# Decoder layer on one core: first copies of the down-projection's weight sums moved to SP's queue in the attention stages, the adding transfers spread singly, the residual loaded in four parts

## The reference

```python
def hybrid_layer(x, ...):
    h = rms_norm(x, norm_mix_pre)
    q, k, v, u, gate_a, gate_s = jnp.split(h @ w_in, IN_SPLITS, axis=-1)
    ...                      # three groups of dilated attention, an S5 state-space branch
    merged = jax.nn.sigmoid(gate_a) * attn_branch + jax.nn.sigmoid(gate_s) * ssm_branch
    x = x + rms_norm(merged @ w_out, norm_mix_post)
    h = rms_norm(x, norm_ffn_pre)
    f = (jax.nn.silu(h @ w_ffn_gate) * (h @ w_ffn_up)) @ w_ffn_down     # D_FF = 5632
    return x + rms_norm(f, norm_ffn_post)
```

## Time and profile before

| | us |
|---|---|
| median of three runs | 2716.58 |
| the profiled execution | 2715.48 |
| its span | 2713.6 |
| PE busy in it | 2629.2 (97%) |
| DVE busy | 1749.2 (64%) |
| ACT busy | 1059.6 (39%) |
| POOL busy | 529.0 (19%) |

### The profile page before, as it was taken

One profiled execution on the slowest core, in us unless ns is written; L12 is line 12 of the kernel. 1 busy time (PEld: TensorE's weight loads), 2 busy tenths in 40 slices (PEclk: granted clock), 3 DMA queues, 4 the chain that ended last, 5 costly groups with the idle time before them and its releaser, 6 DMA issues.

```text
span 2713.6 us, 38844 instructions
## 1 busy us (share of the span) xinstructions
PE 2629.2 (97%) x14213; PEld 2234.7 (82%) x14213; DVE 1749.2 (64%) x2209; ACT 1059.6 (39%) x1427; POOL 529.0 (19%) x825
## 2 busy tenths in 40 slices
PE   8999999999999999999997999999999998999998
PEld 7888888888888888888876878888888887888886
DVE  5333332243345999923756898988989996666677
ACT  5222322233323444522523443434344443555554
POOL 3978037750000000001011110111101000000000
PEclk9999999999999999999998999999999999999999
DMA  6444663344434445466477878778787656777776
GB/s 180 140 144 130 121 194 99 97 120 130 164 123 140 148 139 169 164 220 178 159 222 210 241 205 239 215 210 245 206 241 207 191 170 241 241 241 244 239 242 222
DMA packets 305219, 504.19 MB, mean 186 GB/s; under 512 B 28976, under 2 KB 238256, under 8 KB 302352
## 3 DMA queue, kind: packets, MB, share of 16 engines
q1 hardware_dynamic: 251784, 319.62, 36.5%
q0 software_dynamic: 36032, 164.62, 22.4%
q10 hardware_dynamic: 17288, 18.40, 2.0%
HBM read 448.60 MB, written 150.41 MB: 221 GB/s over the span
## 4 chain that ended last, share of the span: by engine, by line
PE 63%; issue 28%; POOL 4%; DMA 2%; DVE 2%; ACT 1%; ACTq 0%; DVEq 0%; SPq 0%; POOLq 0%
PE ps L494 8%; PE ps L498 8%; PE ps L496 8%; PE ps L785 7%; PE ps L849 5%; PE ps L851 5%; PE ps L853 5%; PE ps L791 3%; POOL v_d L2865 2%; PE ps L615 2%; PE ps L616 2%; PE ps L617 2%; POOL v_d L2862 1%; DMA v_d<-in_w_ffn_down 1%; PE ps L600 1%
## 5 line engine op out<-in xcount | busy, mean ns | idle before, releaser
L482 DVE TENSOR_TENSOR w_lo<-raw,w_hi 128x1024 fp32r<-128x1024 f32 x176 | 229.8, 1306 | 538.2 <-ACT w_hi L478 538.1
L478 ACT ACTIVATE w_hi<-raw 128x1024 fp32r<-128x1024 f32 x176 | 186.4, 1059 | 558.1 <-PE ps L498 346.5
L494 PE MATMUL ps<-a_both,w_hi 128*128 128x512 f32 x640 | 252.3, 394 | 0.0
L496 PE MATMUL ps<-a_both,w_hi 128*128 128x512 f32 x640 | 249.3, 389 | 0.0
L498 PE MATMUL ps<-a_both,w_lo 128*128 128x512 f32 x640 | 249.2, 389 | 0.0
L785 PE MATMUL ps<-a_both,w_hi 128*128 128x512 f32 x872 | 223.7, 399 | 6.0 <-DVE f_sg L2480 5.3
L785 PEld LDWEIGHTS ps<-a_both,w_hi 128*128 128x128 f32 x872 | 163.0, 192 | 41.6 <-issue 7.1
L785 PE MATMUL ps<-a_both,w_hi_b 128*128 128x512 f32 x640 | 163.4, 398 | 3.3 <-ACT w_hi_b L715 2.1
L715 ACT ACTIVATE w_hi<-raw 128x1024 fp32r<-128x1024 f32 x81 | 85.7, 1058 | 185.8 <-DVE raw L2171 82.7
L2891 POOL DMA_DIRECT2D fs_d<-f_sums x22 | 14.0, 637 | 736.9 <-DVE f_sums L2443 736.9
L785 PEld LDWEIGHTS ps<-a_both,w_hi_b 128*128 128x128 f32 x640 | 119.2, 192 | 30.5 <-issue 4.1
(11 more groups left out here) (440 smaller groups left out, 6556.7 us busy)
## 6 DMA issues: line engine op xcount, KB each, us to landing
v_d<-in_w_ffn_down POOLq DMA_DIRECT2D x132, 512.0 KB, 10.0
raw<-in_w_in SPq DMA_DIRECT2D x108, 512.0 KB, 4.1
raw<-in_w_ffn_gate SPq DMA_DIRECT2D x88, 512.0 KB, 18.5
raw<-v_d SPq DMA_DIRECT2D x88, 512.0 KB, 4.8
raw_b<-in_w_ffn_up SPq DMA_DIRECT2D x80, 512.0 KB, 6.0
raw<-in_w_ffn_down SPq DMA_DIRECT2D x66, 512.0 KB, 4.9
v_d<-v_d POOLq DMA_DIRECT2D x44, 512.0 KB, 13.9
raw<-in_w_out SPq DMA_DIRECT2D x32, 512.0 KB, 4.6
```

What stands on the lines that cost most here:

```text
L478: nc.scalar.activation(w_hi[:, m % 2, :], raw[:, m % 4, :], ACT.Copy).then_inc(hi_ready, 1)
L482: nc.vector.tensor_tensor(w_lo[:, m % 2, :], raw[:, m % 4, :], w_hi[:, m % 2, :].bitcast(F32), ALU.subtract).then_inc(lo_ready, 1)
L494: nc.tensor.matmul(o, wh[:, k, cols], x_hi[:, kt0 + k, :], start=first and k == 0, stop=False, skip_group_check=halves)
L496: nc.tensor.matmul(o, wh[:, k, cols], x_lo[:, kt0 + k, :], start=False, stop=False, skip_group_check=halves)
```

## The change

All 88 first copies leave POOL. SP now issues them on its own queue between the loads of q, k, v and of the state-space branch's gated unit, one behind a load. v_d[1] and v_d[3] begin as copies of block(1,1) and block(1,0), and get v_d[0] and v_d[1] added. POOL keeps the 88 adding transfers: turns 0 to 5 every fourth piece of the output projection, none in the first part of the feed-forward layer, turns 6 to 23 behind `store_f_sums(2)` to `store_f_sums(19)`, where each of the four transfers waits for a product of PE of its own. The gain row and the residual are loaded within the down-projection, the residual in four parts of 1 MB. Three pieces in place of four are kept for the end, walked in another order.

```diff
+ENDS = 3
...
-            return sum(2 * (1 <= t <= PAIRS) + (3 <= t < PAIRS + 3) + (5 <= t < PAIRS + 5) for t in range(turns))
+            return sum(2 * (t < PAIRS) + (1 <= t <= PAIRS) + (2 <= t < PAIRS + 2) for t in range(turns))
+
+        def v_begin(sp, i):
+
+            m, (v, j, l) = i // 4, ((0, 0, 0), (2, 0, 1), (1, 1, 1), (3, 1, 0))[i % 4]
+            sp.dma_start(v_d[v][m], w_block(j, l, m)).then_inc(v_begun, 16)
...
-                    for i in range(4):
-                        if c == 0 and d == 0:
-                            pe.wait_ge(lo_ready, B_DN + n + i + 1)
-                            pe.wait_ge(f_lo_ready, F0 + n + i + 1)
...
+            for i in range(ENDS):
+                pe.wait_ge(lo_ready, B_DN + n + i + 1)
+                pe.wait_ge(f_lo_ready, F0 + n + i + 1)
                 for d in range(2):
+                    part(0, d, i)
+            for d in range(2):
+                for i in range(ENDS):
+                    part(1, d, i)
...
                     for k in range(8):
                         load(sp, B_QKV[pr] + 8 * g + k, 0, w_in, 4, 4 * P * (k % 4),
                              512 * g + HQ * (k // 4) + 256 * pr, 256)
+                        if g:
+                            v_begin(sp, 28 * pr + k)
                 for k in range(8):
                     load_wide_v(sp, B_QKV[pr] + 16 + k, 2 * P * k, 2 * HQ + 256 * pr)
+                    v_begin(sp, 28 * pr + 8 + k)
                 for k in range(12):
                     load(sp, B_QKV[pr] + 24 + k, 0, w_in, 4, 4 * P * (k % 4),
                          512 * 2 + HQ * (k // 4) + 256 * pr, 256)
+                    v_begin(sp, 28 * pr + 16 + k)
...
                     load(sp, B_Y0 + 4 * it + k, 0, (w_gv, w_gg)[k // 2], 4, 4 * P * (k % 2), 256 * it, 256)
+                    v_begin(sp, 56 + 4 * it + k)
...
-                dve.wait_ge(x2_back, 16)
+                dve.wait_ge(x2_back, 16 * CLS)
...
-            def v_turn(t):
+            def v_turn(t, pace=None):
 
                 if t:
-                    pool.wait_ge(v_begun, 16 * v_begins(t))
-                if t > 1:
                     pool.wait_ge(v_added, 16 * v_adds(t))
+                else:
+                    pool.wait_ge(v_begun, 16 * 4 * PAIRS)
                 if t < PAIRS:
-                    v_begin(0, t, w_block(0, 0, t))
-                    v_begin(2, t, w_block(0, 1, t))
+                    v_add(0, t, w_block(0, 1, t))
+                    if pace:
+                        pool.wait_ge(product, pace + 2)
+                    v_add(2, t, w_block(1, 1, t))
+                if pace:
+                    pool.wait_ge(product, pace + 7)
                 if 1 <= t <= PAIRS:
-                    v_add(0, t - 1, w_block(0, 1, t - 1))
-                    v_add(2, t - 1, w_block(1, 1, t - 1))
+                    v_add(1, t - 1, v_d[0][t - 1])
+                if pace:
+                    pool.wait_ge(product, pace + 9)
                 if 2 <= t < PAIRS + 2:
-                    v_begin(1, t - 2, v_d[0][t - 2])
-                if 3 <= t < PAIRS + 3:
-                    v_add(1, t - 3, w_block(1, 1, t - 3))
-                if 4 <= t < PAIRS + 4:
-                    v_begin(3, t - 4, v_d[1][t - 4])
-                if 5 <= t < PAIRS + 5:
-                    v_add(3, t - 5, w_block(1, 0, t - 5))
+                    v_add(3, t - 2, v_d[1][t - 2])
...
-            v_turn(0)
-            for t in range(1, 4):
-                pool.wait_ge(piece_done, B_WO + 8 * t)
+            for t in range(6):
+                pool.wait_ge(piece_done, B_WO + 4 + 4 * t)
                 v_turn(t)
...
-            for t in range(4, 6):
-                pool.wait_ge(piece_done, B_FF + 8 * t - 28)
-                v_turn(t)
             for m in range(PAIRS):
                 store_f_sums(m)
-                v_turn(6 + m)
-
-            pool.wait_ge(product, PROD0 + 7 * UNITS)
+                if 2 <= m < PAIRS - 2:
+                    v_turn(m + 4, PROD0 + 14 * m + 85)
+
+            pool.wait_ge(piece_done, B_DN + 30)
             pool.dma_start(gain_o[:, :], A["norm_ffn_post"][0:1, :].partition_broadcast(P)).then_inc(gb_in[1], 16)
-            pool.dma_start(x2_b[:, :, :].rearrange("p c d -> p (c d)"), x2_d).then_inc(x2_back, 16)
+            for c in range(CLS):
+                pool.wait_ge(piece_done, B_DN + 44 + 11 * c)
+                pool.dma_start(x2_b[:, c, :], x2_d[:, D * c:D * c + D]).then_inc(x2_back, 16)
```

More of the change, by code:

```diff
@@ L651, in load_down @@
                 v = {Z5: 0, Z6: 1, Z7: 2, Z4: 3}[q]
-                sp.wait_ge(v_added, 16 * v_adds(m + (2, 4, 2, 6)[v]))
+                sp.wait_ge(v_added, 16 * v_adds(m + (1, 2, 1, 3)[v]))
                 src = v_d[v][m]
@@ L857, in end_pieces, with part @@
         def end_pieces(pe, n):
[L859 removed]
+            def part(c, d, i):
                 toks = slice(c * P, c * P + P)
[L861 to L873 removed]
+                o = down_bank(Z2, c, d)
+                wh = e_hi[:, i, :].rearrange("p (d n) -> p d n", n=512)[:, d, :]
+                wl = e_lo[:, i, :].rearrange("p (d n) -> p d n", n=512)[:, d, :]
+                nc.tensor.matmul(o, ef_hi[:, i, toks], wh, start=False, stop=False, skip_group_check=True)
+                nc.tensor.matmul(o, ef_hi[:, i, toks], wl, start=False, stop=False, skip_group_check=True)
+                mm = nc.tensor.matmul(o, ef_lo[:, i, toks], wh, start=False, stop=i == ENDS - 1, skip_group_check=True)
+                if i == ENDS - 1:
+                    mm.then_inc(down, 1)
+            for i in range(ENDS):
+                pe.wait_ge(lo_ready, B_DN + n + i + 1)
+                pe.wait_ge(f_lo_ready, F0 + n + i + 1)
+                for d in range(2):
+                    part(0, d, i)
+            for d in range(2):
+                for i in range(ENDS):
+                    part(1, d, i)
         def w_tiles(w, row_tiles, rows0, cols0, n):
@@ L1316, in _ @@
                         unit_product(pe, FFN, g, j, p)
-            for n in range(DSTEPS - 4):
+            for n in range(DSTEPS - ENDS):
                 piece_d(pe, n)
-            end_pieces(pe, DSTEPS - 4)
+            end_pieces(pe, DSTEPS - ENDS)
         def act_turn_half(act, h, kts):
@@ L1818, in act_beside @@
                     last_root(i - 10)
-            for n in range(2, DSTEPS - 4):
+            for n in range(2, DSTEPS - ENDS):
                 down_hi(act, n)
                 act_beside(n)
-            for k in range(4):
-                n = DSTEPS - 4 + k
+            for k in range(ENDS):
+                n = DSTEPS - ENDS + k
                 end_split_hi(act, k, B_DN + n)
```

12 lines of the change are left out of this document (4 added, 8 removed).

## The result

The changed kernel takes 2623.9 us (median of 4 runs, 2623.46 to 2625.07) against 2715.67 us for the kernel before on the same chip (4 runs, 2714.59 to 2717.35): a ratio of 0.9662, 95% interval 0.9645 to 0.9679. The forecast was 2630 with a range of 2621 to 2657. The profiled execution took 2625.07 us with a span of 2623.2; that of before had 2713.6, so 90.4 us are to be found. (Of the 6.1 us between forecast and median, 3.9 lie between the sum, 2629.0, and the profiled execution. The rest is that the profiled execution stood 1.1 us under its median before and stands 1.2 above it now.)

What follows compares the result with a forecast made beforehand. PE, busy 97%, bounds the kernel but falls short in places. Gains of 72 us (units), 10.5 (down-projection start) and 4 (end) sum to 86.5: 2715.5 becomes 2629.0, forecast as 2630 us at the median, range 2621 to 2657.

Steps and rivals of the forecast that it cites:

- Turns in the units: Feed-forward units: four transfers fewer per turn, the rest not starting together, return pairs to 38.97 us; 49 us gained, bounds 0 and 49.
- The first two units: First two feed-forward units: no turn runs before the third store, so of 28 us lost all but 5 come back.
- The chain that was to cost 5 us: After 1414.6: ACT and DVE finish f, sums and activation sums before SP can load `raw_b`; 5 us, bounds 0 and 14.
- Start of the down-projection: Gain row and residual come 80 us and more later, 1 MB at a time: 10.5 us gained of a 12 us loss.
- end: Last matmuls: new order of kept pieces avoids two waits and the slow clock behind them; 4 us gained, bounds 0 and 4.5.
- The last low part: At the end: it comes 4.8 us after piece 150 began, PE has 5.4 us of matmuls in hand, so no wait.
- The copies on SP's queue: q, k, v and state-space stages: load and copy need 3.3 of 5.44 us a piece, so 88 copies cost 0.
- The rival of series: SP's queue finishes each transfer before the next, 7.3 us per 5.44 us piece: 2747; 4% slower, 5% for a smaller cost.
- Ahead of the units: Before the feed-forward units: smaller turns in the output projection and copies on SP's queue were each to cost 0.
- the adding transfers are dear: Feed-forward pairs: adding transfers, not their number, do the harm; gate loads land after 14 us, half of 49 stays: 2655; 8%.
- The quarters did not collide: Down-projection: rival that the residual's quarters collide with loads as before, 2.4 us for each MB: 2641; 12%.
- did not hold PE: Feed-forward units: rival that DVE, not the loads, holds PE, so only the ends gain: 2702; 3%.

Runs made afterwards that it cites:

- the delayed pile: Kernel before, each turn of eight transfers from the third store on issued six products later: 2669.39 us; with residual in parts and new end too: 2651.99 us.
- The staircase: Spans from kernel before to changed: 2713.6; turns six products later 2667.5; plus residual in parts, new end 2649.8; copies on SP, additions at old places 2632.8; changed 2623.2.
- two copies: Changed kernel with each of the 88 copies on SP's queue issued a second time into a spare tensor: 2624.33 us.
- three copies: Changed kernel with each of the 88 copies on SP's queue issued three times, two of them into spare tensors: 2700.43 us.

## Why the prediction was right

**The bound and the stages: right.** The four losses that the prediction read from windows and elapsed time are the four that went, and nowhere else did PE gain. Priced by elapsed time the units lost 77.2 us; priced by idle time (21.6 + 30.1) it would have been 52. Not all of the 25 us between them is the clock. A granted clock of 0.82 over 56.5 us and of 0.99 over 621.9 make some 16 of them (an estimate from the earlier trace rows); the rest is not explained.

**Turns in the units: 49 forecast, 47.3 to 48.1 measured** (units 809.2 and 808.4 with the delayed pile against 856.5). The mechanism, pile to gate load to DVE to PE, is shown by the delayed pile, which moves nothing but the moment; DVE's waits for gate loads in the kernel before, 47.7 us in all, are of the same size. The reason given for the changed kernel was only half of it: "the other four no longer start together", one behind the store and one after two more products. The first two do start together, and with all four together the time is the same. What counts is that the pile falls from 18.2 us of the DMA engines to 13.4, under the estimated 15.6 that a gate load may take. And the adding transfers are not "spread singly", as the title of this case has it.

**The first two units: of 28 us, 23 forecast to come back and 5 to stay; 28.3 came (76.4 - 48.1)**, and all 280 products together are 0.9 us over the undisturbed cadence (780.15 against 779.3), with no wait of PE. This is the term that was mis-sized, in the harmless direction, and most of the 4.4 us between its 72 and the 76.4 measured. The chain that was to cost 5 us is there, but faster than assumed. SP's timeline, before and then after:

```profile
1428.15 8.66 SPq L693 DMA_DIRECT2D raw_b<-in_w_ffn_up  x4
1445.09 15.33 SPq L693 DMA_DIRECT2D raw<-in_w_ffn_gate  x4
```

```profile
1421.06 2.02 SPq L695 DMA_DIRECT2D raw_b<-in_w_ffn_up  x4
1430.47 2.04 SPq L695 DMA_DIRECT2D raw<-in_w_ffn_gate  x4
```

The four loads of `raw_b` go out 7 us sooner, take 2.0 us to issue in place of 8.7, and land after 5.9 us in the median (17.3 before), where the prediction allowed 8 from the gate loads of the earlier trace rows, which still had transfers of a turn beside them. ACT waits 0.3 us for them, DVE and PE not at all. The staircase parts the 28: 17 for the copies gone, the rest for the additions out of this stretch.

**Start of the down-projection: 10.5 forecast, 11.2 measured; end: 4 forecast, 3.8 measured.** Each was undone alone, 12.4 and 4.6 us. That no wait comes in four quarters is shown; that the quarters and not their later place avoid it is not, since both were changed together. The last low part still comes late by 0.42 us, at the third kept piece, where the prediction had no wait. The quarters cost nothing: PE has no wait between the 0.45 us at 2201.8 and that one.

**The copies on SP's queue: 0 forecast, and 0.** "The copy, at 3.1 us per MB, 1.6" is 1.4 to 1.5 by the shares, and the rule of the sum (only the share counts, transfers overlap) holds up to a second copy. The rival of series falls with that. By the Trainium skill's formula (DMA: Bandwidth & Descriptors, "Anatomy of one DMA", which gives it for transfers issued by GpSimd; an estimate of 3.2 us for 512 KB) two in series would already cost 1.0 us a piece; the run with load and two copies in 5.44 us speaks against such a use of it, and for what the same page says under "Two DMAs through the same engine are not ordered": descriptors of a queue start in order but are pipelined. The threshold that the prediction gave, a copy holding the queue for 3.7 us, was a fair one: two copies, some 3.0 us, cost nothing, and three, some 4.5, cost 74 us.

**Ahead of the units: 0 forecast, 0.95 us lost in the profiled execution.** In this trace it is one wait of PE in the attention, put down to nothing that the profile shows:

```profile
347.39 0.83 PE L1131 MATMUL ps<-p_t,v_t 128*128 128x128 f32 x6 [0.93 <-issue]
```

The kernels with the end undone and with two copies carry the copies too and have their first unit at 1414.9 and 1414.8, without it; the one without waits for products has it with 1.2 us. The kernel with the residual at once starts its units at 1415.56 without this wait: it is 0.7 us late before 346.3 already, and so is the one with the pile six products later, which has no copies on SP's queue. So a shift of up to 1 us ahead of the units is not tied to the copies. Each kernel has one trace, and whether the wait comes and goes between executions of one kernel is not shown. What it is was not found.

The rivals: the adding transfers are dear (3.0 us against 1.5), as that rival said, yet four of them stay under the lead of the gate load, so its 2655 did not come. The quarters did not collide. DVE was busy for 590.8 of 621.9 us in the stretch of pairs and did not hold PE.

## What to carry to other kernels

When loads of the queue that feeds the bound engine share the DMA engines with bulk work, ask first which load the bulk falls beside and what lead that one has; moving a pile by six products gave 46 us of 90 here for one wait. Price a stretch by elapsed time against its own undisturbed cadence, since matmuls behind a wait can be slower too: here 52 us of idle time were 77 us of loss. Bulk transfers without a deadline belong in a stage whose DMA share is low, and here they cost nothing until load and bulk together took longer than a piece.

## What the runs showed of the hardware

- A transfer of 512 KB that adds into DRAM took about 3.0 us of the 16 DMA engines, a plain copy from DRAM to DRAM 1.5 (estimates from shares of the queue: 0.344 of 39.0 us for four adding ones and a store, 0.348 for eight plain ones and a store).
- Of TensorE's two levels of clock the lower shows behind the wait of 9.77 us in the kernel before: eight matmuls in 3.78 us in place of 2.00, with a granted clock of 0.50 from 1464 to 1466.
- In the stages that carried the copies PE ran without a gap beside DMA shares of 0.93 and 0.99. It lost only when the work of a piece exceeded its 5.44 us: with three copies SP issued a piece in 6.96 us, and 74 us were lost over 88 pieces.
- SP's four issues of a unit's loads, which have no wait between them that could hold, took 2.02 us where no turn was in flight, 8.4 to 9.8 behind four adding transfers at once and 14.1 to 15.3 behind a pile of eight. The issuing engine is held as well as the transfer, so a queue's later loads leave late too:

```profile
1583.11 14.49 SPq L693 DMA_DIRECT2D raw<-in_w_ffn_gate  x4
```

(SP's timeline of the kernel before, in one of the pairs.)
